# Second products of an MLP as seven half-size products with accumulating weight loads

## What is computed

```
hm = rms_norm(x, g_mlp[l])
x = x + jnp.square(jax.nn.relu(hm @ w_up[l])) @ w_down[l]
...
return rms_norm(x, g_final)
```

## Time and profile before

| | us |
|---|---|
| runs of the kernel before | 1572.50, 1573.04, 1575.12 (median 1573.04) |
| the profiled execution's own time | 1572.26 |
| its span (first to last instruction) | 1570.4 |
| TensorE busy | 1526.0 (97%) |
| VectorE busy | 871.3 (55%) |
| ScalarE busy | 715.3 (46%) |
| GpSimd busy | 116.0 (7%) |

### The profile page before, as it was taken

The page is one execution under the profiler, slowest core; times in us unless marked ns, Lnnn a source line. Parts: engine busy times, 40 slices in busy tenths (PEclk is TensorE's granted clock), DMA queues, the critical chain, the costliest instruction groups (busy, mean ns, idle before and its releaser), DMA issues.

```text
span 1570.4 us, 19158 instructions
## 1 busy us (share of the span) xinstructions
PE 1526.0 (97%) x7086; PEld 1234.7 (79%) x7086; DVE 871.3 (55%) x1810; ACT 715.3 (46%) x1630; POOL 116.0 (7%) x121
## 2 busy tenths in 40 slices
PE   7999999999999999999899999999999999999998
PEld 6887778787897777777587878688777888888886
DVE  5467576465465566566447567664555444434344
ACT  6654353333356666665335444443344433324243
POOL 0200000000000004122000005200000000000001
PEclk9999999999999999999999999999999999999999
DMA  6522222323324321112133321234323333333332
GB/s 199 158 68 81 65 70 69 96 78 119 116 81 135 82 63 49 57 54 68 41 121 95 93 59 63 61 114 122 94 81 94 94 96 103 97 94 94 100 102 81
DMA packets 88636, 141.56 MB, mean 90 GB/s; under 512 B 6368, under 2 KB 36448, under 8 KB 88544
## 3 DMA queue, kind: packets, MB, share of 16 engines
q1 hardware_dynamic: 87824, 139.55, 29.3%
q10 hardware_dynamic: 720, 0.80, 0.2%
HBM read 138.23 MB, written 2.10 MB: 89 GB/s over the span
## 4 chain that ended last, share of the span: by engine, by line
PE 80%; DVE 8%; ACT 5%; issue 3%; POOL 2%; DMA 1%; ACTq 0%; POOLq 0%; SPq 0%; DVEq 0%
PE banks L1264 13%; PE banks L1266 12%; PE banks L1265 12%; PE banks L1269 10%; PE banks L1271 10%; PE banks L1270 10%; PE banks L1227 3%; DVE sb_w_split L1969 2%; ACT sb_junk L1534 2%; DVE sb_arena L1969 2%; DVE sb_arena L1978 1%; PE banks L1442 1%; PE banks L1389 1%; ACT sb_w_split L1566 1%; PE banks L1505 1%
## 5 line engine op out<-in xcount | busy, mean ns | idle before, releaser
L1969 DVE TENSOR_TENSOR sb_w_split<-sb_raw,sb_w_split 128x512 fp32r<-128x512 f32 (+4 forms) x530 | 328.5, 661 | 358.0 <-ACT sb_w_split L1566 357.8
L1566 ACT ACTIVATE sb_w_split<-sb_raw 128x512 fp32r<-128x512 f32 (+4 forms) x530 | 288.1, 592 | 400.4 <-PE banks L1266 195.6
L1264 PE MATMUL banks<-sb_actA,sb_w_split 128*128 128x512 f32 x672 | 276.6, 412 | 0.9 <-DVE sb_arena L1969 0.7
L1266 PE MATMUL banks<-sb_actA,sb_w_split 128*128 128x512 f32 x672 | 263.1, 391 | 0.0
L1265 PE MATMUL banks<-sb_actA,sb_w_split 128*128 128x512 f32 x672 | 262.0, 390 | 0.0
L1269 PE MATMUL banks<-sb_w_split,sb_actB 128*128 128x512 f32 (+2 forms) x464 | 181.7, 392 | 0.7 <-DVE sb_actB L1978 0.5
L1271 PE MATMUL banks<-sb_w_split,sb_actB 128*128 128x512 f32 (+2 forms) x464 | 175.9, 379 | 0.0
L1270 PE MATMUL banks<-sb_w_split,sb_actB 128*128 128x512 f32 (+2 forms) x464 | 175.6, 378 | 0.0
L1269 PE MATMUL banks<-sb_w_split,sb_actA 128*128 128x512 f32 (+1 forms) x384 | 152.8, 398 | 10.6 <-DVE sb_w_split L1969 8.8
L1264 PEld LDWEIGHTS banks<-sb_actA,sb_w_split 128*128 128x128 f32 x672 | 126.4, 188 | 30.6 <-issue 5.7
L1264 PE MATMUL banks<-sb_actB,sb_w_split 128*128 128x512 f32 (+1 forms) x384 | 148.8, 387 | 1.4 <-DVE sb_actB L1969 1.4
(11 more groups left out here) (223 smaller groups left out, 2058.3 us busy)
## 6 DMA issues: line engine op xcount, KB each, us to landing
sb_raw<-in_a_w_in SPq DMA_DIRECT2D x66, 256.0 KB, 3.0
sb_raw<-in_w_up SPq DMA_DIRECT2D x32, 512.0 KB, 3.7
sb_raw<-in_w_down SPq DMA_DIRECT2D x32, 512.0 KB, 3.8
sb_raw<-in_w_in SPq DMA_DIRECT2D x24, 512.0 KB, 3.6
sb_raw<-in_mem_w_kv SPq DMA_DIRECT2D x16, 512.0 KB, 3.9
sb_raw<-in_w_ckv SPq DMA_DIRECT2D x16, 512.0 KB, 3.8
sb_raw<-in_a_w_in SPq DMA_DIRECT2D x15, 512.0 KB, 3.7
sb_raw<-in_a_w_out SPq DMA_DIRECT2D x12, 512.0 KB, 3.8
```

Of the source, the lines that this page charges most:

```text
L1264: pe.op.matmul(out, hi[:, cs], x.hi(k), start=i == 0, stop=False)
L1266: t = pe.op.matmul(out, lo[:, cs], x.hi(k), start=False, stop=last_i)
L1566: act.op.activation(hi[:, cs], raw[:, cs], ACT.Copy).then_inc(act.mark(m("w_hi"), 2 * n + part + 1), 1)
L1969: dve.op.tensor_tensor(out, a, b, op).then_inc(dve.mark(*mark) if mark else dve.tick(), 1)
```

## The change

Each block's second product, X (512 tokens x 1024) times W (1024 x 1024), is cut in halves in all three directions and made by seven products of 256 tokens x 512 x 512 (`wn{b}0` to `wn{b}6`, called P1, Q5, P2, P6, Q7, Q3, N4 in their order) in place of eight. Each has 4 k-tiles x 2 token tiles x 3 passes = 24 matmuls of 512 columns, in two chunks of 12.

- **Weights.** Four quarters of the block's `w_down`, 1024 KB each, are fetched by SyncE (`fetchR`). Products Q5, P6, Q7 and N4 need sums of quarters: GpSimd issues a transfer that adds another quarter onto one in SBUF (`tsum`, two of 512 KB for each, eight a block, 32 in all), after the split of the product that used its former content (`w_lo`). A split of such a chunk is one ACT and one DVE instruction 1024 wide, not two of 512.
- **Inputs.** The squared hidden values stay in plain float32 (`f_plain`). DVE makes four differences of quarters in two halves each (`s1`, `ssum`: 8 instructions a block), and the seven inputs are split as `g` (14 ACT and 14 DVE instructions a block; before: 8 and 8).
- **Sums out of the banks.** P1, Q5 and Q7 go to two places (`LANDS`), so that a block has 20 DVE instructions for its banks (before: 8). What belongs to two quarters for good is kept in `first_sum` and added at the end by three steps `fix` of two instructions.
- **Norm factor.** It is applied in the first product's eviction (`nrow` brings it as a row by four transposes on PE, and the maximum becomes one fused instruction); `esum` is gone.
- **Columns of `up`.** A chunk of `w_up` comes as two transfers of 256 columns. Eight banks are used in turn.
- **End.** The four token tiles are closed after Q3 (tiles 0, 1) and after N4 (tiles 2, 3).

The diff, cut:

```diff
+WINO_ORDER = (P1, Q5, P2, P6, Q7, Q3, N4)
+WEIGHT = {P1: 0, Q5: 0, P6: 0, N4: 0, Q7: 1, P2: 2, Q3: 3}
+ADDED = {Q5: 1, P6: 3, Q7: 3, N4: 2}
...
-            add(f"up{b}{g}", ("w_up",), D_MODEL, [(b * D_MODEL + g * 512, 512)], "feature", "hE", "relu")
-        for half in range(2):
-            add(f"dn{b}{half}", ("w_down",), D_MODEL, [(half * 512, 512)], "token", f"f{b}", "tok", k0=b * D_MODEL)
+            add(f"up{b}{g}", ("w_up",), D_MODEL, [(b * D_MODEL + g * 256 + c, 256) for c in (0, 512)], "feature", "hE", "relu")
+        for i in range(7):
+            add(f"wn{b}{i}", None, 512, [(0, 512)], "token", f"F{b}{i}", "wn" if len(LANDS[i]) == 1 else "wn2",
+                tokens=SEQ // 2)
...
-    p.side(0, (), ("nsq", "e"), ("esum",), lag=4000)
+    scales(0, "e", after=[("sqp", "e", 7)])
...
+        if b:
+            p.soon.extend([[("fetchR", b, i)] for i in (1, 0, 2, 3)] + [[("tsum", b, Q7, 0)], [("tsum", b, Q7, 1)]])
...
+        work = {P1: [[("tsum", b, Q5, 1), ("s1", b, 1)], [("g", b, Q3, 0)], [("g", b, Q5, 1)], [("tsum", b, P6, 0)]],
+                Q5: [[("g", b, P2, 1), ("tsum", b, P6, 1)], [("ssum", b, 2, 1)], [], []],
+                P2: [[("g", b, P6, 1)], [("ssum", b, 3, 1)], [], []],
+                P6: [[("g", b, Q7, 1), ("tsum", b, N4, 0)], [("ssum", b, 4, 1), ("tsum", b, N4, 1)], [], []],
+                Q7: [[("g", b, Q3, 1)], [], [], []], Q3: [[("g", b, N4, 1)]], N4: []}
...
+        if b == 3:
+            work[Q3] += [[("fix", 0)], [("fix", 1)], [("fix", 2)],
+                        [(kind, *([1] if kind == "fsq" else []), j) for j in (2, 3) for kind in ("fsq", "fg")]]
...
+                if i in ADDED:
+                    act.wait_ge(m(f"dma_sum{i}{c}"), 16 * (b + 1))
+                else:
+                    act.wait_ge(m(f"dma_quarter{WEIGHT[i]}"), 16 * (b + 1))
+                act.wait_ge(*m.chunk_done(n - SPLIT_SLOTS))
+                act.op.activation(hi, raw, ACT.Copy).then_inc(act.mark(m("w_hi"), 2 * n + 2), 2)
...
+        elif kind == "tsum":
+            b, i, c = a
+            if i == Q7:
+                pool.wait_ge(m("dma_quarter1"), 16 * (b + 1))
+            else:
+                pool.wait_ge(*m.wino_split(b, {Q5: P1, P6: Q5, N4: P6}[i], c))
+            r0, c0 = b * D_MODEL + 512 * (ADDED[i] // 2) + 256 * c, 512 * (ADDED[i] % 2)
+            pool.op.dma_start(v.wino_weight(i, c), v.io["w_down"][r0:r0 + 256, c0:c0 + 512].rearrange("(k p) n -> p k n", p=P),
+                              accum_op=ALU.add).then_inc(m(f"dma_sum{i}{c}"), 16)
```

## The result

| | before | after |
|---|---|---|
| median of 15 runs, us | 1573.34 (1570.40 to 1575.42) | 1576.37 (1573.94 to 1578.76) |
| ratio | | 1.0022, 95% interval 1.0014 to 1.0029 |
| profiled execution's own time / span | 1572.26 / 1570.4 | 1575.62 / 1573.8 |

The kernel became 3.0 us slower where 11 us less were forecast; 1576.4 lies outside the range. Lines are those of the changed kernel. First its page, part 1, which answers to the first line of the earlier trace rows: PE is busy for 14.3 us less, but DVE for 85 us more.

What follows compares the result with a forecast made beforehand. TensorE, busy for 97% of the span, was taken to bound the kernel. The terms -21.8 + 0.4 + 1.6 + 0 + 7.0 + 2.1 gave -10.7 us, forecast 1562 us, range 1554 to 1574 (the forecast's own 1557 to 1567).

Steps and rivals of the forecast that it cites:

- the schedule of DVE: Start of the second products: DVE's steps laid out from P1 as time 0, Q5's first chunk split by 3.5 us.
- +1.6 us of waits: PE's waits for DVE in the second products: 0.4 us a block, range 0 to 8 us in all.
- 0.5 of slack: Second products: smallest distance, in us, between DVE finishing a chunk's split and PE needing it.
- Removed matmuls: Second products: 96 fewer matmuls of 0.2267 us each, -21.8 us, all on the path.
- DVE's load: Second products of a block: DVE busy for 34.6 of 38.1 us, 91%.
- Accumulating transfers: Sums of weight quarters: X, from the releasing split to landing, about 6.5 us; up to 7.3 costs nothing, so 0 us.
- The end: Behind the last matmul: four closings in a row on DVE, +7.0 us, and collisions with POOL, +2.1 us.
- half of four collisions: Last block: POOL's `fg` lengthening DVE's work, up to 4 x 1.03 us, of which half was taken, +2.1.
- Rival 1: Sums land late at Q5, X beyond 7.3 us, PE waits in every block: up to 1579 us; chance 0.14.
- Rival 2: Second products: POOL's issues of transfers lock DVE, +8 to +14 us, about 1572 us; chance 0.09.
- Its second form: DVE instructions keep GpSimd from writing descriptors, so X grows to 7.6: +1.3 us in all, 1563 us.
- Rival 3: At the end, closings overlap better without collision cost, adding only 3.7 us: 1555 us; chance 0.12.

Runs made afterwards that it cites:

- e1: From the changed kernel, g of P6's first half and ssum 4 moved ahead of the split of P1's second chunk: 1568.2 us.
- e3: From the changed kernel, P1 lands once instead of twice, its two subtractions into first_sum left out, order kept: 1572.0 us.
- e9: From e6, no gain products on POOL or ACT scalings of first halves; DVE scales a whole tile in one 1024-column instruction: 1559.8 us.
- e10: e8 with POOL's first two gain products done on one column instead of 512: 1574.8 us.
- e2: From the changed kernel, the accumulating transfers overwrite instead, so the sums of quarters are left out: 1576.4 us.
- e11: e9 with the accumulating transfers overwriting instead, so the sums of quarters are left out: 1559.5 us.
- e6: The order of e5_order2 together with the paired closings of e4: 1563.7 us.
- e7: From the changed kernel, POOL's gain products of tiles 2 and 3 done on one column instead of 512: 1574.9 us.
- e8: From the changed kernel, last block only: squares and gain products of P2's tiles behind P6's second chunk, first fix behind N4's last split: 1578.1 us.
- e4: From the changed kernel, DVE does sum and mean of both tiles of a pair ahead of their scalings at the end: 1573.8 us.
- e5_order2: e1 plus earlier g of P1's second half, g of Q3's first half moved to Q7, and the last-block order of e8: 1566.1 us.

## Why the prediction was wrong

**The step that failed** is the schedule of DVE: "The last bank of `up` is full at 0; DVE 0.6, ACT's square to 1.3, its split of Q5's first chunk to 2.4; DVE's part to 3.5", and the term built on it, +1.6 us of waits. The trace has 4.2, 4.8, 5.8 and 7.1: the lateness is all there at the first entry, and comes from the order ahead of it. I started the clock at P1 and took DVE as free there. Ahead of it the order has an eviction, a `g`, an `ssum`, an eviction, a `g`: each `g` needs ACT, and ACT needs the eviction just made. The rows of the order stood before me; I did not lay out the 3 us in front of time 0. Everything behind was right and shows the same distance: P2's first chunk ends at P1+13.6 (forecast 9.95), P6's at P1+19.5 (15.85), 3.6 us late each, since a DVE forecast at 91% and measured at 89% makes nothing good. 3.6 less the 0.5 of slack is 3.1 us, about what PE waits in a block. e1 (8.9 us of waits gone by two steps moved) and e3 show both halves of this, and in e9, whose order no longer has this lateness, PE waits 0.8 us in all, less than the 1.6 of the forecast. The term was 14.6 us, beyond its stated range of 8.

Second, in the last block 1.9 us of these were not foreseen at all: two `fsq` stand ahead of the split of Q7's first chunk in ACT's queue and wait until DVE has taken P2's bank (1.3 us of PE's time), and a `fix` stands ahead of N4's last split (0.6). e10, which moves both, has 1.9 us less.

```profile
1536.70 0.64 ACT L1642 ACTIVATE sb_junk<-sb_arena 128x512 f32<-128x512 f32 x1 [4.58 <-DVE sb_arena L2094]
```

**The other terms**, against the trace:
- Removed matmuls, -21.8: right; a block is 81.6 us plus its waits.
- DVE's load, 34.6 us of 38.1: 34.0 busy in the window shown. The prices were right.
- Accumulating transfers, X taken 6.5 and no cost: 6.1 from issue to landing, and some 0.45 from the split's end to the issue (1341.44, 1341.89), 6.5 in all. e2 and e11 find no cost in the time; the traces show 0.8 us of PE's waits behind a late sum in e9, and 1.7 in e6. From the Trainium skill ("DMA: Bandwidth & Descriptors", "Bandwidth") I had estimated 3.4 us of plain transfer plus emission and landing; e2's rows say 4.6 in all.
- The end, +7.0 and +2.1: measured 12.9 - 3.5 = 9.4. Right in size: DVE's Q3 closing starts at E-3.2 (forecast -3.6), the collisions cost 2.1 (e7). That half of four collisions was the right share was luck: the first pair of `fg` cost nothing only because DVE rested there in the wait nobody had foreseen; beside a split it costs 2.9 (e8).
- Sum with the measured terms: -21.8 + 0.4 + 14.6 + 0 + 9.4 = +2.6; the two profiled executions are 3.4 apart, and 0.8 stay unassigned.

**Rivals.** Rival 1 (sums land late) named the right place, Q5, and the wrong cause for this kernel: e2. It shows, small, once the order is good (block 2 of e6 and e9). Rival 2 (POOL's issues hold DVE up) is refuted by the rows of an issue on POOL and of DVE beside it, which keeps its 0.68 and 1.22. Its second form, X grown to 7.6 by waits for DVE, doesn't show either: X is 6.5 with DVE 89% busy.

```profile
1351.73 1.21 POOL L2703 DMA_DIRECT2D sb_arena<-in_w_down  x1 [8.62 <-DVE sb_w_split L2149]
```

```profile
1351.88 0.68 DVE L2094 TENSOR_TENSOR sb_actB<-sb_arena,sb_actB 128x512 fp32r<-128x512 f32 x1
1352.48 1.22 DVE L2149 TENSOR_TENSOR sb_w_split<-sb_arena,sb_w_split 128x1024 fp32r<-128x1024 f32 x1
```

Rival 3's better end (E+7.0) did not come, not even with the closings paired: E+9.7 in e4. That the order at the boundary would be late was no rival of mine, and the chance of 0.79 for faster rested on one schedule whose first entry was assumed.

## What to carry to other kernels

When engines work in order, a table of due times has to start where the first of its engines was last idle, not where the stage starts: lay out the evictions and what stands between them, and look for a step that needs another engine's answer to the eviction just made. With an engine about 90% busy behind that point, nothing of such a round trip is made good: beyond the slack it is paid in full, in pieces at the next hand-overs. So put these steps where that engine rests anyway (here half a chunk earlier: 8 us for two moved entries). And before moving a GpSimd product to a calmer place in the list, look what VectorE does there.

## What was not expected of the hardware

- A DVE instruction with two inputs from SBUF can lose to *two* POOL products in a row: 4.15 us for 1.22 (e8_last, and 4.16 in e5_order2), 1.22 again without them (e10_last2). At the end of the changed kernel another such pair cost 1.0 and 1.1, as the scaling that began 0.06 us behind POOL was done at 1561.95, 1.1 us before POOL was. Why it got through there and the split did not stays open. The Trainium skill ("SBUF — State Buffer", "two separate sides") has an exclusive lock for the whole of one instruction; the rows agree with the blocking, but a loss of both products together is more than one instruction.
- Adding costs an issued transfer of 512 KB 1.5 us: 6.1 against 4.6 us on the same queue (after, e2_plain), 0.5 of it in the issue on POOL (1.2 against 0.72).
- A wait of PE costs 0.11 us beyond itself: the next matmul starts 0.34 us after the first one behind the wait, not 0.23 (1351.41, 1351.75, and at nearly every wait of the changed kernel).
- After a wait of 1.9 to 2.0 us the clock fell in one of three cases (e6_both). Why there and not in the others stays open.
